# A hybrid decoder step on one core: attention of tiles 3 to 7 begins 2 to 10 slots later, one head more is streamed, three gates are moved

## The reference, cut to what matters

```python
# x: 1024 prompt rows + 32 sample rows, D = 1024, all float32
proj = rmsnorm(x) @ w_in                      # q, k, v (4 heads), u (pooling input)
attn = softmax(q1 k1) v - lam * softmax(q2 k2) v     # causal, with a bias by distance
attn = rmsnorm(attn, subln_g)
pool_out = (window means of u - u) @ pool_w   # windows 2, 4, 8, 16
x = x + concat(attn, pool_out) @ w_out        # "x1"
# PEER: 8 heads, each with two sets of 128 keys
s = (rmsnorm(x) @ wq) . sub_keys ; top 16 of 16 x 16 pairs -> idx (16 experts), softmax -> gate
h = gelu(xn . u_tab[idx]) ; x = x + sum_k gate*h * v_tab[idx]      # "x2"
x = x + sigmoid(rmsnorm(x) @ w_gate) * (p @ w_pl)                  # the gate
y = rmsnorm(x, final_g)
```

## Time and profile before

| | |
|---|---|
| three runs, median | 3151.11 us |
| the profiled execution | 3152.38 us, its span 3150.3 us |
| PE, VectorE, ScalarE, POOL busy | 74%, 71%, 30%, 42% of the span |
| moved | 1258.70 MB, 1133.76 MB of it gathered by POOL |
| mean rate | 400 GB/s |
| granted TensorE clock, mean | 0.867 |

### The profile page before, as it was taken

How to read it: one execution, slowest core, us unless ns; L and a number is a source line. 1 busy time by engine, 2 the same in 40 slices (tenths; PEclk the granted TensorE clock), 3 DMA queues, 4 the chain that set the end, 5 groups by cost and what they waited for, 6 DMA issues and landing times.

```text
span 3150.3 us, 53247 instructions
## 1 busy us (share of the span) xinstructions
PE 2340.0 (74%) x20870; PEld 928.2 (29%) x20870; DVE 2224.2 (71%) x5420; ACT 953.4 (30%) x2436; POOL 1324.5 (42%) x1143
## 2 busy tenths in 40 slices
PE   7889998577877887757876667576777676667656
PEld 3643333233333333213431222122222121222112
DVE  1376767678868789656667667587777777777775
ACT  0422233334425345222322222132332332232222
POOL 1034434333434344345655544344444444444452
PEclk9999999788988988868878878798898897889778
DMA  7699999999999999999999999999999999999996
GB/s 251 232 371 421 421 407 420 417 405 391 406 401 418 409 395 420 415 408 417 416 417 411 416 415 398 418 415 419 405 419 408 420 415 421 404 420 416 420 414 270
DMA packets 201110, 1258.70 MB, mean 400 GB/s; under 512 B 23892, under 2 KB 27244, under 8 KB 59924
## 3 DMA queue, kind: packets, MB, share of 16 engines
q0 software_dynamic: 159808, 1133.76, 87.5%
q1 hardware_dynamic: 39616, 121.25, 10.1%
q10 hardware_dynamic: 1436, 0.29, 0.0%
HBM read 1226.74 MB, written 28.65 MB: 399 GB/s over the span
## 4 chain that ended last, share of the span: by engine, by line
DMA 30%; PE 15%; DVE 7%; POOL 3%; issue 2%; DVEq 2%; ACT 2%; POOLq 0%; ACTq 0%
DMA ring<-in_uv,idx 30%; PE sc L1018 7%; DVE ring L1888 4%; PE sc L1051 3%; POOL ring L2108 3%; PE route L993 2%; PE sc L1020 1%; DVEq L1898 1%; ACT diag L1414 1%; PE sc L1011 0%; ACT hgelu L1409 0%; PE sc L715 0%; PE sc L917 0%; PE sc L887 0%; DVE x L1937 0%
## 5 line engine op out<-in xcount | busy, mean ns | idle before, releaser
L2108 POOL DMA_INDIRECT ring<-in_uv,idx x1056 | 1245.2, 1179 | 1631.1 <-PE sc L1020 1403.2
L1018 PE MATMUL sc<-ring,diag 32*32 32x512 f32 x8192 | 1241.1, 726 | 676.3 <-ACT diag L1414 630.2
L1888 DVE CUSTOM_DVE_ANT_0 ring<-ring,xn_cur 128x1024 f32<-128x1024 f32 x1056 | 1280.2, 1222 | 635.0 <-DMA ring<-in_uv,idx 628.4
L1020 PE MATMUL sc<-ring,diag 32*32 32x512 f32 x8192 | 1240.5, 726 | 0.0
L1018 PEld LDWEIGHTS sc<-ring,diag 32*32 32x32 f32 x8192 | 272.0, 118 | 1458.9 <-ACT diag L1414 1051.9
L1409 ACT ACTIVATE hgelu<-hdot 128x2 f32<-128x2 f32 x528 | 107.5, 204 | 1815.5 <-DVE hdot L1888 1814.9
L1414 ACT ACTIVATE diag<-gate_d,hgelu 128x32 f32<-128x32 f32 x1056 | 281.7, 314 | 21.2
L1020 PEld LDWEIGHTS sc<-ring,diag 32*32 32x32 f32 x8192 | 271.1, 118 | 0.6 <-issue 0.6
L575 PE MATMUL sc<-big,front 128*128 128x512 f32 x384 | 176.8, 603 | 2.4 <-DVE front L1517 2.4
L1409 ACT ACT_TABLE_LOAD x129 | 165.5, 1283 | 2.3
L993 PE MATMUL route<-big,xnT 128*128 128x256 f32 x560 | 134.1, 393 | 0.0
(11 more groups left out here) (307 smaller groups left out, 2346.8 us busy)
## 6 DMA issues: line engine op xcount, KB each, us to landing
front<-wqk_scratch SPq DMA_DIRECT2D x21, 1024.0 KB
ring<-in_uv,idx POOLq DMA_INDIRECT x1056
big<-in_w_in SPq DMA_DIRECT2D x8, 1024.0 KB, 13.4
wqk_scratch<-front SPq DMA_DIRECT2D x8, 1024.0 KB, 5.0
big<-wqk_scratch SPq DMA_DIRECT2D x8, 1024.0 KB, 20.1
x<-x_scratch SPq DMA_DIRECT2D x12, 512.0 KB
ring<-in_wq_t POOLq DMA_DIRECT2D x10, 512.0 KB, 33.6
front<-in_x SPq DMA_DIRECT2D x8, 512.0 KB, 7.0
```

Of the source, the lines that this page charges most:

```text
L1018: pe.matmul(sc[own, 0, :], diag[own, r, :], uv_rows[own, place, D:D + W4], start=opens_sum, stop=closes).then_inc(row_added[r], 1)
L1020: pe.matmul(sc[other, 1, :], diag[own, r, :], uv_rows[own, place, D + W4:2 * D], start=opens_sum, stop=closes).then_inc(row_added[r], 1)
L1888: dve.tensor_tensor_reduce(uv_rows[:, row_of(k), 0:D], uv_rows[:, row_of(k), 0:D], xn_cur[:, :], 1.0, 0.0, ALU.mult, ALU.add, hdot[:, n % ...
L2108: pool.indirect_dma_start(uv_rows[:, row_of(k), :], None, uv, bass.IndirectOffsetOnAxis(ap=idx[:, n % PH, j:j + 1], axis=0)).then_inc(row_ ...
```

## The change

Three tables of numbers:

```diff
-STREAMED = 29
+STREAMED = 30
...
-    b = {2: 67, 3: 84, 4: 101, 5: 123, 6: 145, 7: 167}[t]
+    b = {2: 67, 3: 86, 4: 105, 5: 129, 6: 153, 7: 177}[t]
...
-GATE_JOBS = [(4, 322), (0, 342), (3, 361), (5, 384), (1, 404), (6, 448), (2, 468), (7, 512)]
+GATE_JOBS = [(4, 329), (0, 347), (3, 365), (5, 384), (1, 404), (6, 448), (2, 468), (7, 512)]
```

## The result

Measured side by side, the changed kernel took 3159.98 us (median of 13 runs, 3154.65 to 3164.15) and the kernel before 3152.23 (13 runs, 3148.71 to 3157.91 but for one of 3963.8, which the ratio leaves out). The ratio is 1.0023, 95% interval 1.0016 to 1.0031: 7.3 us slower, where 4.5 us faster was forecast, and above the range's 3158. Run again in another set, the same kernel came to 3159.2 and 1.0023 [1.0014, 1.0032].

The account below looks back on a forecast made before the run. Transfer bytes were taken to set the time, with gaps where TensorE's queue delays row sums at tile starts. Terms -8 - 1 + 2.5 + 3 + 1 - 2 = -4.5 gave 3146.6 us by the median; range 3137 to 3158.

Parts of the forecast that it names:

- A: Starts of tiles 3 to 7: two free slots after the last half projection relieve TensorE; -8 us, bounds -13.0 to 0.
- PE's lateness: At tile starts: TensorE work beyond 2.6 us spare a slot, added up slot by slot; 10.7 to 14.5 us a tile.
- B: Inside tile 3, VectorE the limit: -1 us (-3 to +2); tile 6's norm at slot 160: 0 (-1.7 to +2).
- C: One streamed head more, a 1024 KB transfer: +2.5 us with a full queue, 0 if it fills missing time.
- D: Openings of tiles 2, 3 and 4 at slots 128, 192, 256, partly covered: +3 us, from 0 to 8.3.
- E: First three gates 18 slots apart: waits for x2 cost +1 (0 to 12.6); last steps clear of the norm, -2.
- F: Whole sample stage 10 slots later beside the same gathers, projections at slots 311 and 313: 0 us (-2 to +2).
- 1: Rival: the tile starts lose nothing any more, A -13; -14.8 us in all, 3136.3 us; chance 0.15.
- 2: Rival: projections alone empty the queue, turn and band add little, A 0; +4.5 us, 3155.6 us; chance 0.17.
- rival 3: TensorE's clock falls in the free slots; turn, band and routing 8.1 us longer; +3.5 us, 3154.6 us; chance 0.04.
- 4: Rival: x2's reload at gates 347 and 365 stops transfers, 6.3 us each; +8.3 us, 3159.4 us; chance 0.10.

## Why the prediction was wrong

**A, the starts (-8, bounds -13 to 0): right, and a little too small.** By five slots from each start on, 13.6 us became 3.3 and 4.8; with tile 5's part of the hole at 128 left aside, some 11 to 12 of them went. Its reason, PE's lateness, bears out roughly and not tile by tile. Tile 4, whose turn follows right behind the projection even in the kernel after, was given 0.2 us of relief and got 2.2 and 1.1. In the run with every start one or two slots later, tile 5 is late by 4.5 + 5.7 + 0.5 = 10.7 us in the prediction's count, as much as tile 7 before, and missed nothing where that missed 2.8. That the move off the routing of slot 122 did this is likely and was not tested.

**B, inside the tiles (-1 and 0): the step that failed.** The prediction saw tile 6's norm at slot 160, priced it by the 1.7 us that it missed before, and gave it +2 at the most. It cost 5.7 us more over slots 156 to 167. The shift moved a middle head's exponentials ahead of the root of the norm in slot 162 on ScalarE, and the wait for that root, which no term of the sum had, started the chain at slot 164: with the norm two slots later 1.1 us are missing there in place of 7.3. No row of before showed it, only the order of ScalarE's queue. Tile 3, for which -1 was taken, missed 2.3 us more in slots 92 to 98 (3.2 over 92 to 99 in the mean of both profiles), for the most part not at the norm that I had named (slots 96 to 98, 2.2 us in place of 0.9) but at slots 93 to 95 (5.8 in place of 2.0).

**C, the streamed head (+2.5):** 1 us by the run without it, with 2.5 inside the interval: not settled, though slots 192 to 223 over all profiles speak for some 1 us as well.

**D, the openings (+3 in all, 0 to 8.3):** the kind was right and the places were not. Slot 192 missed 0.2 and 1.1 us in the two profiles, slot 256 0.1 and 0.2, and 128 alone 4.9 and 5.5. The prediction had written that projections 126 and 127 stand right ahead of it, but priced it by the opening at 448 (2.8 us), which has none ahead. A block of 7.1 us ahead of an add of 3.5 us adds up, as PE and VectorE wait for each other in turn (6.50 and 4.71 us); with slot 127 free between them 0.0 us were missing, and 1.8 in two other kernels.

**E, the gates (-1): right in the sum.** Alone they gave -1.6 us by the medians and -0.3 by the ratio, neither clear of nothing. The waits before L1949 were 2.71 and 2.57 us, not the 6.3 that the term was worked out from, at 419 and 416 GB/s.

**F, the samples' stage (0): right**, 1.0000 with it alone, though slots 300 to 319 miss 6.3 us in place of 4.2. But tile 7's own end across slot 192, which neither F nor D named, missed 2.2 us more in slots 192 to 223 in the mean; the later end as a whole, with its megabyte and the relief of tile 7's start in it, cost 4.1 us.

The sum with what the two profiles show in the mean (the table, with the 3.2 us of tile 5's start taken out of slots 124 to 131): A -10.8, B +3.2 and +5.7, C +2.5 at full rate, D +5.0, slots 192 to 319 +3.0, the gates -0.9, all other slots -0.8, together +6.9 for a forecast of -4.5. The difference is B (9.9 us), D (2), the end (3), and A (3) the other way. The size of single terms is good to 1 or 2 us, by the scatter of the rows above.

Of the rivals, 1 was right on the starts and wrong on all else. 2 is refuted at the starts: tile 7's projections of 7.1 us, with two slots of row sums between them and its turn, empty nothing. The samples' two halves, alone in their slots, still go with missing time, and no run shows why. 3 is refuted as a cause: the granted clock was 1.00, its upper level of 2.4 GHz, in the windows shown behind all five starts, behind the two free slots of tiles 6 and 7 too. It was at the lower level at one start, tile 5's, in slot 129 (0.50), where PE had stood idle for 4.71 us; the turn took 0.9 us more for it, in place of the 8.1 us of rival 3, and in the kernel with tile 4 at 104 the same slow turn went with nothing missing. The Trainium skill's rule (TensorE: Matmul & The Clock Gate, "HAM oscillation — how this bites in real kernels"), that idle gaps of PE let the clock fall, agrees with slot 129; it did not decide the time. 4 came out near the measured time (3159.4) by a cause that was not there: that is luck. None of them was what happened, so the fault was in the range as well: the prices came from windows in which the jobs stood apart, and no case was kept for two of them falling together.

What stays open: how exactly the end's 4 us divide between tile 7's last head and the streamed megabyte, what makes the hole in slot 156 and the samples' part, and why the same spacing is worth 4 us more one or two slots earlier, which the missing time of the profiles does not show.

## What to carry over

When a timetable is shifted against jobs that stay, don't price only the place that is relieved: for each fixed job, engine by engine, what now stands in the same slot ahead of it and behind it, above all where an engine with little work (ScalarE here, 30% busy) sits between two others. As slot 164 shows, a hole of 7 us can open with no engine overloaded, from three waits of about 3 us in a row. And where a relief of 11 us shows up in the windows but not in the time, look for the slots that got worse, move one job by a slot or two, and measure again: two such repairs gave back 4 to 6 of 7.3 us, and choosing the phase of the whole timetable gave 4 to 5 us below before.

## What the runs showed of the hardware

- A load of ScalarE's table takes 1.28 us. Slot 162 of the kernel after has three of them (gelu, root, gelu), 3.8 us in a slot whose quiet length is 5.1, and the exponentials' stands just ahead. The Trainium skill (ScalarE: Activation LUTs, "What ACT_TABLE_LOAD costs") gives 1283 ns for the load, and the trace agrees; the page adds a drain of about 1380 ns to every switch, and the trace does not agree with that: the root began at 1134.46, 1.29 us behind the start of its load at 1133.17, and that load 0.02 us behind the end of the instruction before it.
- The opening's add takes 0.69 us for 128x512 and 2.77 us for the other half of x in four pieces of 32x512 (L1937): each piece costs as much as the whole 128x512.
- Two profiles of one kernel differed by 6.5 us in span (3152.6 and 3159.1), spread over small differences at many slots; the two big holes stood in both (7.3 and 6.8 us at slots 164 and 165, 4.9 and 5.5 at 128 to 130).
- Behind 4.71 us without work PE's granted clock was 0.50 in slot 129, and the same eight products of the turn took 1.96 us in place of 1.04.
